# Projections of later heads in two attention mixers: seven products of quarters inside the attention loops

## What is computed

```python
def nsa_moba_mixer(x, ...):                       # layer 0: "first mixer"
    proj = x @ w_in
    qa, kc, vc, ksl, vsl, kw, vw, ga, qm, km, vm = jnp.split(proj, EVEN_SPLITS, axis=-1)
    ...
    o_b = moba_attention(rope(heads(qm, MOBA_HEADS), positions),
                         rope(heads(km, MOBA_HEADS), positions), heads(vm, MOBA_HEADS))
    return jnp.concatenate([o_a, o_b], axis=-1) @ w_out

def stick_breaking_mixer(x, w_in, w_out):         # layer 1: "second mixer"
    q, k, v = jnp.split(x @ w_in, 3, axis=-1)
    heads = lambda a: a.reshape(B, S, SB_HEADS, HEAD_DIM)
    return stick_breaking_attention(heads(q), heads(k), heads(v)) @ w_out
```

## Time and profile before

| what | value |
|---|---|
| median of 3 runs | 1143.73 us (1143.28 to 1144.44) |
| the profiled execution, its own time | 1144.65 us |
| its span in the trace | 1142.9 us |
| PE busy | 1058.1 us, 93% |
| DVE busy | 401.9 us, 35% |
| ACT busy | 221.1 us, 19% |
| POOL busy | 1.0 us |
| mean granted clock of TensorE | 0.984 of full speed |

### The profile page before, as it was taken

One profiled execution on the slowest core, in us unless ns is written; L12 is line 12 of the kernel. 1 busy time (PEld: TensorE's weight loads), 2 busy tenths in 40 slices (PEclk: granted clock), 3 DMA queues, 4 the chain that ended last, 5 costly groups with the idle time before them and its releaser, 6 DMA issues.

```text
span 1142.9 us, 15878 instructions
## 1 busy us (share of the span) xinstructions
PE 1058.1 (93%) x6490; PEld 527.8 (46%) x6490; DVE 401.9 (35%) x1070; ACT 221.1 (19%) x509; POOL 1.0 (0%) x6
## 2 busy tenths in 40 slices
PE   9999999999999999999999999987878897789996
PEld 6555455554786455554655544423222332224231
DVE  5776463114556654114736734101100010001003
ACT  2045341111024432111131522101000000001011
POOL 0000000000000000000000000000000000000000
PEclk9999999999999999999999999999988999899999
DMA  9878478977943378996836738999999999999995
GB/s 320 185 199 292 174 266 357 421 329 251 339 163 132 122 275 346 421 381 208 322 130 228 290 136 290 386 430 425 428 429 426 428 430 427 428 430 428 399 424 231
DMA packets 84997, 363.66 MB, mean 318 GB/s; under 512 B 23138, under 2 KB 28612, under 8 KB 61892
## 3 DMA queue, kind: packets, MB, share of 16 engines
q1 hardware_dynamic: 84132, 362.59, 81.3%
q10 hardware_dynamic: 800, 0.17, 0.1%
HBM read 361.69 MB, written 1.05 MB: 317 GB/s over the span
## 4 chain that ended last, share of the span: by engine, by line
PE 67%; DMA 23%; DVE 6%; ACT 1%; issue 1%; SPq 1%; DVEq 0%
DMA weights<-in_expert_w_down_dram 16%; PE bank L1471 13%; PE bank L1025 6%; PE bank L1003 6%; PE bank L1535 5%; PE bank L1583 5%; DMA weights<-in_expert_w_up_dram 4%; PE bank L1515 4%; PE bank L1684 3%; PE bank L1015 2%; PE bank L1812 2%; PE bank L1403 2%; PE bank L1957 2%; PE bank L1242 2%; DMA weights<-in_expert_w_gate_dram 1%; PE bank L1917 1%
## 5 line engine op out<-in xcount | busy, mean ns | idle before, releaser
L1471 PE MATMUL bank<-weights,mixed 128*32 128x512 f32 x992 | 226.3, 610 | 31.3 <-DMA weights<-in_expert_w_gate_dram 17.9
L1471 PEld LDWEIGHTS bank<-weights,mixed 128*32 128x32 f32 x992 | 63.1, 112 | 181.1 <-issue 169.6
L1025 PE MATMUL bank<-weights,mixed 128*128 128x512 f32 x192 | 89.8, 602 | 0.0
L1003 PE MATMUL bank<-weights,x_transposed 128*128 128x512 f32 x192 | 89.2, 601 | 0.0
L1535 PE MATMUL bank<-weights,work 128*32 128x512 f32 x464 | 62.1, 670 | 25.5 <-DMA weights<-in_expert_w_down_dram 21.0
L3098 DVE TENSOR_TENSOR work<-work,bank 64x512 f32<-64x512 f32 (+1 forms) x22 | 15.0, 682 | 157.7 <-PE bank L1471 156.0
L2285 ACT ACTIVATE work<-bank 128x512 f32<-128x512 f32 (+1 forms) x32 | 19.0, 594 | 229.5 <-PE bank L1535 190.7
L3000 DVE COPY work<-bank 64x512 f32<-64x512 f32 (+1 forms) x30 | 20.7, 690 | 117.0 <-PE bank L1535 75.1
L1684 PE MATMUL bank<-work,heads_transposed 128*128 128x512 f32 x120 | 56.0, 607 | 4.6 <-ACT work L2285 4.6
L1471 PE MATMUL bank<-weights,projected 128*64 128x256 f32 x512 | 57.0, 381 | 0.0
L3005 DVE COPY work<-bank 128x256 f32<-128x256 f32 (+1 forms) x22 | 10.8, 493 | 127.4 <-PE bank L1487 127.4
(11 more groups left out here) (464 smaller groups left out, 1405.8 us busy)
## 6 DMA issues: line engine op xcount, KB each, us to landing
weights<-in_expert_w_gate_dram SPq DMA_DIRECT2D x28, 2048.0 KB, 16.9
weights<-in_expert_w_up_dram SPq DMA_DIRECT2D x28, 2048.0 KB, 17.7
weights<-in_expert_w_down_dram SPq DMA_DIRECT2D x24, 2048.0 KB, 19.1
weights<-in_moe_w_down_dram SPq DMA_DIRECT2D x16, 2048.0 KB, 14.7
weights<-in_moe_w_gate_dram SPq DMA_DIRECT2D x14, 2048.0 KB, 13.0
weights<-in_moe_w_up_dram SPq DMA_DIRECT2D x12, 2048.0 KB, 15.2
weights<-in_sb_w_in_dram SPq DMA_DIRECT2D x6, 2048.0 KB, 19.5
weights<-in_w_in_dram SPq DMA_DIRECT2D x6, 2048.0 KB, 16.2
```

The costliest lines, as they stand in the source:

```text
L1003: i = mm(BANK[bank or 6 + t][:, :], XT[:, kt, t * P:(t + 1) * P], w[:, kt, :], start=kt == 0, stop=kt == KT - 1)
L1025: i = mm(BANK[bank][:, :], mixT[:, kt, t * P:(t + 1) * P], w[:, kt, :], start=kt == 0, stop=kt == KT - 1)
L1471: i = mm(b[n_slots * c:n_slots * (c + 1), e * F:(e + 1) * F], x[:, kt, q * n_slots:(q + 1) * n_slots], extra_weights(c, kt) if outside els ...
```

## The change

For the two chunks of queries and keys in each mixer, the four quarter products per output half (eight in all) are replaced by seven products of quarters, built on sums and differences of quarters of the inputs and of the weights. A quarter product is here 128 tokens by 512 rows of weights by 512 columns: four matmuls of 128x512 in the first mixer (`pieces`), or sixteen of 128x128 in the second (`second`).

- The seven products take the places of the projection pieces: in the first mixer four before the loop and half of the fifth, `product_6`; the other half of it, `product_7` and `product_4` in steps 0 to 7; the values start at step 8 and have two, two, one and one matmul in steps 10 to 13. In the second mixer the products stand in steps 0 to 6, and the values move to steps 7, 8, 10 and 11; step 9 has no filler.
- The sums of weights (128x2048 each, in place in the slots) are four on DVE in the first mixer (`MW1` to `MW4`: three before the loop, `MW4` in step 0) and four on POOL in the second (`VS1` to `VS4`). The sums of the inputs are the ones that the mixers' first projections already form; they are kept in another buffer, `NORM_`, which moves two loads of norm parameters later on SP (into the expert stage, after its third chunk).
- The products are put together by 128x512 additions on DVE: seven in each mixer (`after_product_...`, `after_second_...`); ACT copies three products in each out of the accumulator (`AU`, `qm0`, `qm1`; `copy_4`, `copy_1`, `copy_5`). ACT's former copies of these projections are gone.
- `rope_moba(3, 0)` moves from before the loop into step 4, `rope_moba(3, 1)` from step 5 to 6.
- `moba_heads(5)` on PE waits for the last addition (`proj_copied` 5, in DVE's step 8); the values' first half in the second mixer waits for the addition in DVE's step 7 (`proj_copied` 11).

```diff
+        Q1_LO, Q1_HI = (slot(N_SB + 3)[:, at:at + HALF_SLOT] for at in (0, HALF_SLOT))
+        K1_LO, K1_HI = (slot(N_SB + 4)[:, at:at + HALF_SLOT] for at in (0, HALF_SLOT))
+        VS1, VS2, VS3, VS4 = K1_HI, Q1_LO, K1_LO, Q1_HI
...
+        KM_LO, KM_HI = (slot(N_AB + 4)[:, at:at + HALF_SLOT] for at in (0, HALF_SLOT))
+        QM_LO, QM_HI = (slot(N_AB + 5)[:, at:at + HALF_SLOT] for at in (0, HALF_SLOT))
+        MW1, MW2, MW3, MW4 = QM_LO, QM_HI, KM_LO, KM_HI
...
@@ gpsimd
+            for n in (N_SB + 3, N_SB + 4):
+                pool.wait_ge(slot_loaded[n % NSLOT], loaded_value(n))
+            pool.wait_ge(half_psum, 4)
+            nc.gpsimd.tensor_tensor(VS1, K1_LO, K1_HI, ALU.add).then_inc(pool_filled, 1)
+            pool.wait_ge(half_psum, 5)
+            pool.wait_ge(pool_filled, 2)
+            nc.gpsimd.tensor_tensor(VS3, Q1_LO, K1_LO, ALU.subtract).then_inc(pool_filled, 1)
+            pool.wait_ge(pool_filled, 3)
+            nc.gpsimd.tensor_tensor(VS2, VS1, Q1_LO, ALU.subtract).then_inc(pool_filled, 1)
+            pool.wait_ge(products_psum, AB_PRODUCTS + 3)
+            pool.wait_ge(pool_filled, 4)
+            nc.gpsimd.tensor_tensor(VS4, Q1_HI, VS2, ALU.subtract).then_inc(pool_filled, 1)
...
@@ tensor
-                         (N_SB + 5, 0): (half_copied, 5), (N_SB + 5, 1): (proj_copied, 11)}
+            HALF_FREE = {(N_AB + 6, 0): (sums_ready, 11), (N_AB + 6, 1): (qt_act, 7),
+                         (N_SB + 5, 0): (proj_copied, 11), (N_SB + 5, 1): (sums_ready, AB_SUMS + 6)}
...
-            project_half(N_AB + 4, 0, 0, 4)
+            def pieces(bank, x, weights, k0=0, k1=KT // 2):
+                w = quarter(weights)
+                for kt in range(k0, k1):
+                    i = mm(BANK[bank][:, :], x[:, kt, :], w[:, kt, :], start=kt == 0, stop=kt == KT // 2 - 1)
+                return i
+            def product_6(k0, k1):
+                if k0 == 0:
+                    pe.wait_ge(half_copied, 2)
+                    pe.wait_ge(sums_ready, 6)
+                i = pieces(6, AS[1], MW2, k0, k1)
...
+            pe.wait_ge(proj_copied, 1)
+            chunk_loaded(N_AB + 4)
+            pieces(6, lo[:, :, 0:P], KM_LO).then_inc(half_psum, 1)
...
-            project_half(N_AB + 4, 0, 4, 8)
+            pieces(7, hi[:, :, 0:P], KM_HI).then_inc(products_psum, 1)
...
+                pieces(6, AS[3], QM_HI, 3, 4).then_inc(half_psum, 1)
+                pe.wait_ge(sums_ready, 5)
+                pieces(7, AS[0], MW1).then_inc(products_psum, 1)
...
-            project_half(N_AB + 5, 0, 0, 2)
+            product_6(0, 2)
             pe.wait_ge(qt_act, 3)
             attention(AB_JOBS, 0, 0, {
-                0: lambda: project_half(N_AB + 5, 0, 2, 3),
-                1: lambda: (cmp_keys(), project_half(N_AB + 5, 0, 3, 5)),
-                2: lambda: (cmp_score(), project_half(N_AB + 5, 0, 5, 7)),
-                3: lambda: project_half(N_AB + 5, 0, 7, 8),
-                4: lambda: (project_half(N_AB + 5, 1, 0, 2), cmp_transpose()),
-                5: lambda: project_half(N_AB + 5, 1, 2, 3),
-                6: lambda: project_half(N_AB + 5, 1, 3, 5),
-                7: lambda: project_half(N_AB + 5, 1, 5, 6),
-                8: lambda: project_half(N_AB + 5, 1, 6, 8),
+                0: lambda: product_6(2, 3),
+                1: lambda: (cmp_keys(), product_6(3, 4)),
+                2: lambda: (cmp_score(), product_7(0, 2)),
+                3: lambda: product_7(2, 3),
+                4: lambda: (product_7(3, 4), cmp_transpose()),
+                5: lambda: product_4(0, 1),
+                6: lambda: product_4(1, 2),
+                7: lambda: product_4(2, 4),
+                8: lambda: project_half(N_AB + 6, 0, 0, 2, 7),
                 9: lambda: moba_heads(5),
-                10: lambda: (project_half(N_AB + 6, 0, 0, 2, 7), moba_heads(6)),
-                11: lambda: project_half(N_AB + 6, 0, 2, 4, 7),
-                12: lambda: (project_half(N_AB + 6, 0, 4, 6, 7), moba_heads(7)),
-                13: lambda: (project_half(N_AB + 6, 0, 6, 8, 7), moba_heads(8)),
+                10: lambda: (project_half(N_AB + 6, 0, 2, 4, 7), moba_heads(6)),
+                11: lambda: project_half(N_AB + 6, 0, 4, 6, 7),
+                12: lambda: (project_half(N_AB + 6, 0, 6, 7, 7), moba_heads(7)),
+                13: lambda: (project_half(N_AB + 6, 0, 7, 8, 7), moba_heads(8)),
...
+            def second_5():
+                pe.wait_ge(half_copied, 5)
+                pe.wait_ge(pool_filled, 2)
+                second(7, VS1, XS[0]).then_inc(products_psum, 1)
+            def second_6():
+                pe.wait_ge(sums_ready, AB_SUMS + 4)
+                pe.wait_ge(pool_filled, 4)
+                second(6, VS2, XS[1]).then_inc(products_psum, 1)
+            def second_7():
+                pe.wait_ge(proj_copied, 10)
+                second(7, VS3, XS[2]).then_inc(products_psum, 1)
+            def second_3():
+                pe.wait_ge(sums_ready, AB_SUMS + 5)
+                pe.wait_ge(pool_filled, 5)
+                second(6, VS4, hi[:, :, P:S]).then_inc(chunk_done, 2)
...
             sb_filler = {
-                0: lambda: project_half_T(N_SB + 3, 0, 0, 8), 1: lambda: project_half_T(N_SB + 3, 0, 8, 16),
-                2: lambda: project_half_T(N_SB + 3, 1, 0, 8), 3: lambda: project_half_T(N_SB + 3, 1, 8, 16),
-                4: lambda: project_half_T(N_SB + 4, 0, 0, 8), 5: lambda: project_half_T(N_SB + 4, 0, 8, 16),
-                6: lambda: project_half_T(N_SB + 4, 1, 0, 8), 7: lambda: project_half_T(N_SB + 4, 1, 8, 16),
-                8: lambda: project_half(N_SB + 5, 0, 0, 4), 9: lambda: project_half(N_SB + 5, 0, 4, 8),
+                0: second_4, 1: second_1, 2: second_2, 3: second_5, 4: second_6, 5: second_7, 6: second_3,
+                7: lambda: project_half(N_SB + 5, 0, 0, 4), 8: lambda: project_half(N_SB + 5, 0, 4, 8),
...
@@ scalar
-            take_moba_half(3, 1)
-            attention(AB_JOBS, 0, {2: cmp_exponent, 4: lambda: (take_moba_half(4, 0), cmp_pT_copy()), 9: lambda: (take_moba_half(4, 1), moba_heads(5)),
+            act.wait_ge(half_psum, 2)
+            ac(pj[:, 0, C_QM:C_QM + CH], BANK[6][:, :], ACT.Copy).then_inc(half_copied, 1)
+            act.wait_ge(products_psum, 7)
+            ac(pj[:, 1, C_QM:C_QM + CH], BANK[7][:, :], ACT.Copy).then_inc(proj_copied, 1)
...
+            sb_copies = {1: copy_4, 2: copy_1, 4: copy_5, 10: lambda: take_sb_half(0), 12: lambda: take_sb_half(1)}
...
@@ vector
+            tt(km0, AU, BANK[7][:, :], ALU.add)
+            weights_loaded(N_AB + 4)
+            weights_loaded(N_AB + 5)
+            tt(MW1, QM_LO, KM_LO, ALU.subtract).then_inc(sums_ready, 1)
...
-            rope_moba(3, 0)
+            dve.wait_ge(sums_ready, 5)
+            dve.wait_ge(half_psum, 2)
+            tt(MW2, QM_HI, MW1, ALU.subtract).then_inc(sums_ready, 1)
...
+            tt(MW3, MW2, KM_LO, ALU.subtract).then_inc(sums_ready, 1)
+            def after_product_5():
+                dve.wait_ge(half_copied, 2)
+                dve.wait_ge(proj_copied, 4)
+                tt(qm0, qm0, BANK[7][:, :], ALU.add).then_inc(sums_ready, 1)
+                tt(MW4, MW2, KM_HI, ALU.subtract).then_inc(sums_ready, 1)
+            def after_product_6():
+                dve.wait_ge(products_psum, 8)
+                link(tt(AU, AU, BANK[6][:, :], ALU.add))
+                tt(qm0, qm0, AU, ALU.add).then_inc(sums_ready, 1)
...
+            def after_product_4():
+                dve.wait_ge(chunk_done, N_AB + 6)
+                tt(km1, AU, BANK[6][:, :], ALU.subtract).then_inc(proj_copied, 1)
...
-            attention(AB_JOBS, 0, 0, {1: keys_copy, 2: cmp_softmax_in, 3: cmp_softmax_out, 5: lambda: rope_moba(3, 1), 7: lambda: rope_moba(4, 0),
-                                      10: lambda: rope_moba(4, 1),
+            attention(AB_JOBS, 0, 0, {0: after_product_5, 1: keys_copy, 2: lambda: (cmp_softmax_in(), after_product_6()), 3: cmp_softmax_out,
+                                      4: lambda: rope_moba(3, 0), 5: after_product_7, 6: lambda: rope_moba(3, 1), 7: lambda: rope_moba(4, 0),
+                                      8: after_product_4, 10: lambda: rope_moba(4, 1),
...
+            def after_second_6():
+                dve.wait_ge(products_psum, AB_PRODUCTS + 5)
+                link(tt(U2, U2, BANK[6], ALU.add))
+                dve.wait_ge(proj_copied, 10)
+                tt(second_q[:, :, P:S], second_q[:, :, P:S], four(U2), ALU.add).then_inc(sums_ready, 1)
+            def after_second_7():
+                dve.wait_ge(products_psum, AB_PRODUCTS + 6)
+                link(tt(U2, U2, BANK[7], ALU.add))
+                tt(second_k[:, :, P:S], second_k[:, :, P:S], four(U2), ALU.add)
+                tt(second_k[:, :, 0:P], second_k[:, :, 0:P], four(U2), ALU.add).then_inc(sums_ready, 1)
+            def after_second_3():
+                dve.wait_ge(sums_ready, AB_SUMS + 5)
```

(3 more changed lines are left out.)

117 lines of the change are left out of this document (87 added, 30 removed).

## The result

The changed kernel takes 1173.56 us (median of 5 runs, 1172.34 to 1174.16) against 1143.73 before: +29.8 us, a ratio of 1.026 (95% interval 1.0245 to 1.0275). The forecast was slower by 8.4, with a range that ended at 1159. The sign was right, the size was not: more than two thirds of the loss was not in the sum.

A forecast was written before the change was run, and what follows sets the result against it. The prediction took PE to bound both mixers' loops, with DVE having time to spare. First mixer +5.6, second mixer +1.4 and POOL's sums +1.4 made +8.4 on the median 1143.73, so 1152.1 us, range 1147 to 1156 (outer 1145 to 1159).

The forecast's parts named there:

- What bounds the kernel: Both mixers' loops: PE bounds them at full clock, DVE has 6 and 20 us to spare, shifts count one to one.
- First mixer, +5.6: First mixer's loop: DVE's 8.7 us of new work exceeds 4.58 idle; `scores(10)` +7.3, saved matmuls give back 1.72.
- Second mixer, products and the wait at the values, +1.4: Second mixer's loop: seven products save 3.4 us, PE waits 4.8 at the values for DVE's addition in step 7.
- steps 0 to 6 keep their times: Second mixer's loop: each product takes 3.57 us, about as long as a filler, so these steps do not shift.
- GpSimd, +1.4: Second mixer: three POOL sums of 5.1 us against 13.9 available make PE wait 1.4 us at `second_6`.
- The rival that was nearest: Second mixer: DVE stretches POOL's sums to 7.4 us, PE waits 8.3 at `second_6`, 1159.0 us; chance 0.16.
- the saving doesn't pass through: Rival for both mixers that it does: DVE's idle time absorbs its new work, 6.8 us gained, 1136.9; chance 0.13.
- Small terms all fall low: Rival: first mixer +2.4, values' wait no more than the products save, no POOL wait; 1146.1 to about 1143; chance 0.08.

The follow-up runs named there:

- first_only: Kernel before with the seven products in the first mixer alone, second mixer as before: 1150.56 us, +6.5, ratio 1.0056.
- no_mw4: Changed kernel without the sum `MW4` in DVE's step 0 of the first mixer; the fourth product uses the weights as they are: 1170.14 us.
- best_second: Kernel before plus second mixer's seven products, sums on VectorE (three before loop, one in step 3), values in a free bank, ACT copies a step earlier: 1141.25 us.
- sums_on_dve: Changed kernel with the second mixer's four sums of weights on VectorE (steps 1, 3, 3 and 5), none on GpSimd: 1162.37 us.
- second_only: Kernel before with the seven products in the second mixer alone, first mixer as before: 1165.14 us, +21.1, ratio 1.019.

## Why the prediction was wrong, step by step

**What bounds the kernel:** right. PE bound both loops, DVE had the room, and the change moved work from the one that bounds to the other. Shifts passed to the end nearly one to one (30.2 at the end of the second loop, 28.9 at the end of the span).

**First mixer, +5.6:** right; 6.5 by `first_only` (4.6 to 8.4 by its interval). `product_6` waits 0.96 for ACT's copy (0.94 forecast); `scores(10)` stands at 96.74 (95.9) and waits where it was said to, at `moba_heads(5)` behind the addition of step 8 (1.58 idle at 94.95). Counted from the first scores, at 61.79, it comes 34.95 us later, where the prediction has 33.73 (62.17 to 95.9). The term that was missing is the lower clock: the compressed scores took 1.4 more, DVE idled 2.52 for them where 1.05 was forecast, and `no_mw4` gives back 3.4 for a sum of 2.28. The prediction read a clock of 1.00 in the windows of before and kept it for a loop in which PE would wait.

**Second mixer, products and the wait at the values, +1.4:** the wait was 4.57, 4.8 forecast. The saving was mis-sized: -2.5 measured, -3.4 forecast. The 25.01 us for seven products come from products in a row ahead of the loop; in the chain of `best_second` three of them take 3.57 in the loop and four, those behind scores, 3.77. Not foreseen: behind the wait the values ran at the lower clock (6.47 for 3.6), and ACT's copy of the second half, moved to step 12, cost 2.52. And "steps 0 to 6 keep their times" failed, by the next term.

**GpSimd, +1.4:** this is the step that failed. Its bounds were 1.8 and 5.1 us, its measured time 4.5, and PE never waited for the sums; by that the term should have been about 0 (the third sum ended 17.65 us behind the loop's first filler, and the place of `second_6` is 17.44 behind it), and the figure of the Trainium skill's page "GPSIMD Engine Reference", which the prediction set beside it, was right. But the step asked only when the sums would be ready for PE. It put what they do to the engine beside them at nothing. They held DVE for 14.0 us (12.57 at the scans, 1.44 at the softplus) in the place where its chain sets the pace of the loop. PE waited 10.40 for that chain and 1.71 at `copy_1` behind it, and most of the lower clock went with the hold in `sums_on_dve` (6.3 of 7.8). The second loop as measured: 12.1 for the hold, 4.57 and 2.52 of waits, 7.8 of lower clock, less 2.5 saved and less the 0.9 that PE idled before too, makes the 23.6; the prediction had 2.8.

**The rival that was nearest** had the two engines meet and priced it the wrong way round: GpSimd slowed by VectorE to 7.4 us, PE waiting 8.3 at `second_6`, 1159. In the trace GpSimd's sums kept their 4.5 us and VectorE stood. The range ended at that rival, so the time fell outside it. The prediction had cited the sentence on contention; who is held, and for how long, stands on another page of the Trainium skill, "SBUF — State Buffer", section "Who interferes with whom", that it had not weighed. Taken from there and priced by a page's 4.5 us a sum, the four sums would have stood in the sum as up to 18 us, an estimate from these pages.

**The other rivals:** the saving doesn't pass through in either mixer as the change was written. `best_second` shows that it can in the second one, 2.7 us, when no sum runs beside two-operand work and no bank is waited for. In the first mixer no such place was found: moving `MW4` gave back 2.2 to 3.3 of 6.5. *Small terms all fall low* wanted 2.4 in the first mixer, and that one cost 6.5.

**What is open:** when the clock comes back. After equal waits it came back at once in one kernel and some us later in another (1.95 and 3.75 for the same four records), worth some 2 us there. No run here settles it.

## What to carry to other kernels

Before work is put on an idle engine, list what the neighbours do in the same stretch and which operands they read: a GpSimd sum over 2048 columns was free beside VectorE work that reads a bank, and held one VectorE instruction with two SBUF operands for up to its whole length. Put such sums where VectorE idles or reads banks; cutting them into four gave back only 4.9 of 29.8 us. And where PE, which bounds a loop at full clock, is made to wait a few microseconds, count the slower matmuls that may come behind the wait as well as the wait.

## What the runs showed of the hardware that I had not expected

- A two-operand VectorE instruction (scan, softplus) beside a GpSimd sum ends just behind the sum: 4.6 us instead of 0.42, one such instruction for each sum. With one SBUF operand and a bank it kept its time (masks 1.02 for two, additions 0.69); beside GpSimd clearings, which read nothing, a softplus took 0.56.
- Pieces of 512 columns hold nearly as much in sum: about 12 us instead of 14.0. Four pieces take GpSimd 5.27 to 5.62 us for the columns that one sum did in 4.55; the first three pieces took 1.27 or 1.28 each, all but one of the later ones 1.37 to 1.60.
- Waits of PE of 1.4 to 10 us were often followed by matmuls at about half speed: 6.47 us for what takes 3.60, granted clock 0.54 to 0.73 in those stretches, where the kernel before had 1.00 throughout both loops. Not always: behind a wait of 1.53 in the first loop of `no_mw4` the granted clock stayed 1.00, and so it did behind 2.55 in `second_only`.
